# The ten pairs of score maps of a tile in another order in an fp32 transformer trunk kernel

## What is computed

```
def attend(q, k, v):
    s = einsum('bqhgd,bkhd->bhgqk', q, k) * dk ** -0.5
    p = softmax(s, axis=-1)
    return einsum('bhgqk,bkhe->bqhge', p, v)

o_a = attend(q_a, k_a, v_a)                  # 6 heads, 64 wide
o_g = attend(q_g, k_g, v_g)                  # 6 heads, 64 wide
o1 = attend(q_d[..., 0, :], k_d[..., 0, :], v_d)   # 4 differential heads,
o2 = attend(q_d[..., 1, :], k_d[..., 1, :], v_d)   # two maps of 32 each
o_d = rms_norm(o1 - lam * o2, diff_g) * (1.0 - lam_init)
x = x + gate1 * (concat(o_a, o_g, o_d) @ w_out)
```

## Time and profile before

| | |
|---|---|
| median of 3 executions | 1749.79 us (1747.08 to 1751.12) |
| profiled execution: its own time | 1749.15 us |
| its span in the profile | 1747.3 us |
| TensorE matmul busy | 1529.3 us, 88% of the span |
| VectorE busy | 728.0 us, 42% |
| ScalarE busy | 422.4 us, 24% |
| mean granted clock of TensorE | 0.93 |

### The profile page before, as it was taken

One profiled execution on the slowest core, in us unless ns is written; L12 is line 12 of the kernel. 1 busy time (PEld: TensorE's weight loads), 2 busy tenths in 40 slices (PEclk: granted clock), 3 DMA queues, 4 the chain that ended last, 5 costly groups with the idle time before them and its releaser, 6 DMA issues.

```text
span 1747.3 us, 20005 instructions
## 1 busy us (share of the span) xinstructions
PE 1529.3 (88%) x7010; PEld 836.2 (48%) x7010; DVE 728.0 (42%) x1671; ACT 422.4 (24%) x919; POOL 235.2 (13%) x368
## 2 busy tenths in 40 slices
PE   5999988999979899999988998889998975999970
PEld 0134444577756524445523444457776653444430
DVE  0004433567743323344432443356774433433335
ACT  0110111666620001111122111166662000111112
POOL 5111100000020012311031110000002000111114
PEclk8999988799999899999998999879999986999995
DMA  9950008000040478999998000300003006999954
GB/s 313 343 210 11 1 0 277 1 1 2 1 157 29 176 266 262 373 383 382 323 348 315 11 0 1 97 1 2 2 1 109 35 27 219 341 367 368 366 178 183
DMA packets 151834, 283.07 MB, mean 162 GB/s; under 512 B 7104, under 2 KB 95392, under 8 KB 146736
## 3 DMA queue, kind: packets, MB, share of 16 engines
q1 hardware_dynamic: 126832, 197.41, 33.5%
q0 software_dynamic: 24896, 84.28, 12.8%
HBM read 244.45 MB, written 37.32 MB: 161 GB/s over the span
## 4 chain that ended last, share of the span: by engine, by line
PE 76%; DVE 9%; DMA 6%; issue 4%; ACT 2%; POOL 1%; DVEq 1%; SPq 0%; POOLq 0%; ACTq 0%
PE ps L1556 16%; PE ps L1832 16%; PE ps L1501 9%; PE ps L1517 8%; PE ps L1855 7%; PE ps L1631 6%; PE ps L1684 5%; PE ps L1749 4%; DMA ring<-in_w_mod 3%; DMA arena<-in_norm_g 2%; DVE ring L1172 2%; PE ps L1771 1%; PE ps L1626 1%; ACT hT_region L812 1%; PE ps L1578 1%
## 5 line engine op out<-in xcount | busy, mean ns | idle before, releaser
L1556 PE MATMUL ps<-ring,hT_region 128*128 128x512 f32 (+1 forms) x640 | 283.7, 602 | 27.8 <-ACT hT_region L812 27.8
L1832 PE MATMUL ps<-ring,hT_region 128*128 128x512 f32 x624 | 277.6, 598 | 2.0 <-DVE hT_region L1434 1.7
L1556 PEld LDWEIGHTS ps<-ring,hT_region 128*128 128x128 f32 x640 | 125.9, 200 | 167.4 <-issue 166.4
L1517 PE MATMUL ps<-ring,silu_c 128*2 128x512 f32 x384 | 177.4, 624 | 32.4 <-DMA ring<-in_w_mod 29.1
L1172 DVE TENSOR_SCALAR_CACHE_REDUCE ring<-ps 128x768 f32<-128x768 f32 (+1 forms) x168 | 132.7, 820 | 120.3 <-PE ps L1631 97.5
L1832 PEld LDWEIGHTS ps<-ring,hT_region 128*128 128x128 f32 x624 | 116.8, 192 | 135.4 <-issue 135.4
L1749 PE MATMUL ps<-ring,hT_region 128*128 128x384 f32 (+1 forms) x480 | 146.1, 462 | 0.0
L880 ACT ACTIVATE ring<-ring,negm 128x768 f32<-128x768 f32 (+1 forms) x168 | 137.7, 820 | 33.5 <-DVE ring L1172 33.5
L1855 PE MATMUL ps<-arena,work 128*128 128x512 f32 x312 | 140.5, 593 | 1.4 <-DVE work L1457 1.4
L1631 PE MATMUL ps<-arena,qT 64*128 64x384 f32 (+1 forms) x640 | 128.7, 521 | 10.4 <-DVE ring L1172 5.7
L1441 DVE TENSOR_SCALAR work<-work 128x256 f32<-128x256 f32 x39 | 11.5, 294 | 260.0 <-ACT work L966 260.0
(11 more groups left out here) (260 smaller groups left out, 1595.9 us busy)
## 6 DMA issues: line engine op xcount, KB each, us to landing
ring<-in_w_mod SPq DMA_DIRECT2D x24, 2048.0 KB, 12.4
ring<-in_moe_w_gate SPq DMA_DIRECT2D x39, 1024.0 KB, 11.5
ring<-in_moe_w_up SPq DMA_DIRECT2D x39, 1024.0 KB, 13.5
arena<-in_moe_w_down SPq DMA_DIRECT2D x39, 1024.0 KB, 7.9
y_rows<-arena POOLq DMA_DIRECT2D x39, 512.0 KB, 7.9
ring<-in_w_in SPq DMA_DIRECT2D x6, 2048.0 KB, 9.6
arena<-mod_rows POOLq DMA_DIRECT2D x16, 512.0 KB, 11.0
y_rows<-x POOLq DMA_DIRECT2D x1, 7680.0 KB, 21.9
```

The source lines that it names most:

```text
L1517: last = mm(ps[0:2, 2 + j % 2, :], silu_v[:, :, c], w[:, c, :], start=(c == 0), stop=(c == KC - 1))
L1556: last = mm(ps[:, b, 0:n], hT[:, c, t * P:(t + 1) * P], w[:, c, :], start=(c == 0), stop=(c == KC - 1))
L1832: last = mm(ps[:, 2 + i % 2, :], hgT[i % 2][:, c, :], w[:, c, :], start=(c == 0), stop=(c == KC - 1))
```

## The change

The position in the loop and the number of the pair are no longer the same. A table `ORDER` says which pair stands at which position: 0, 6, 1, 2, 3, 7, 4, 8, 9, 5. Pairs 6 and 8, which form no unit of their own, now stand at positions 1 and 7 (before: 6 and 8). The units follow the positions 0, 2, 3, 4, 5, 6, 8, 9 (before: 0 to 5, 7, 9). `COL_OF` says which columns of the output a unit fills. ScalarE's copy of the first four outputs moves by one turn, since the fourth unit comes one turn later.

```
+ORDER = [0, 6, 1, 2, 3, 7, 4, 8, 9, 5]
-UNIT_OF = {0: 0, 1: 1, 2: 2, 3: 3, 4: 4, 5: 5, 7: 6, 9: 7}
+UNIT_OF = {0: 0, 2: 1, 3: 2, 4: 3, 5: 4, 6: 5, 8: 6, 9: 7}
+COL_OF = [0, 1, 2, 3, 6, 4, 7, 5]
+DIFF_UNITS = [u for u in range(N_U) if COL_OF[u] >= 6]
...
-                    if p == 7:
+                    if p == 8:
                         out_copy(t, 0)
...
-                    if p in (6, 8):
+                    if pair in (6, 8):
                         to = dbuf[:, 0:n]
-                        if p == 8:
-                            dve.wait_ge(pt_done[min(t, 1)], units_before(l, t, 6, min(t, 1)) + 1)
+                        if pair == 8:
+                            dve.wait_ge(pt_done[min(t, 1)], units_before(l, t, DIFF_UNITS[0], min(t, 1)) + 1)
...
-                    if k >= 1 and (k - 1) % N_PR >= 6:
+                    if k >= 1 and ORDER[(k - 1) % N_PR] >= 6:
                         difference(k - 1)
...
-                    if p < 6:
+                    if ORDER[p] < 6:
                         pe.wait_ge(exp_done, l * NS + 2 * k + 2)
                         ab = pr[k % 3]
                     else:
-                        pe.wait_ge(d_ready, l * 4 * NT + 4 * t + p - 5)
+                        pe.wait_ge(d_ready, l * 4 * NT + 4 * t + ORDER[p] - 5)
                         ab = [dbuf, pr[k % 3][0]]
...
-                        if p == 9 and b == 0:
+                        if u == 7 and b == 0:
                             pe.wait_ge(oT_ready, l * NT + t)
```

More of the change, by code:

```diff
@@ L878, in probs @@
                     v = pr[k % 3][m][:, 0:P if t == 0 else 768]
-                    c = MAPS * (t % 2) + 2 * p + m
+                    c = MAPS * (t % 2) + 2 * ORDER[p] + m
                     act.activation(v, v, ACT.Exp, bias=negm[:, 2 * (k % 3) + m:2 * (k % 3) + m + 1], scale=-1.0,
@@ L1171, in row_max @@
                         o_ = pr[k % 3][m].rearrange("p (a n) -> p a n", a=2)
-                    ts(o_, i_, -pair_of(p)[4], None, ALU.mult, ALU.min, accum_out=col).then_inc(m_ready, 1)
+                    ts(o_, i_, -pair_of(ORDER[p])[4], None, ALU.mult, ALU.min, accum_out=col).then_inc(m_ready, 1)
                 def probsT(k):
@@ L1185, in difference @@
                     n = P if t == 0 else 768
-                    c = MAPS * (t % 2) + 2 * p
+                    pair = ORDER[p]
+                    c = MAPS * (t % 2) + 2 * pair
                     dve.wait_ge(exp_done, l * NS + 2 * k + 2)
@@ L1193, in difference @@
                     to = p1
-                    if p in (6, 8):
+                    if pair in (6, 8):
                         to = dbuf[:, 0:n]
-                        if p == 8:
-                            dve.wait_ge(pt_done[min(t, 1)], units_before(l, t, 6, min(t, 1)) + 1)
+                        if pair == 8:
+                            dve.wait_ge(pt_done[min(t, 1)], units_before(l, t, DIFF_UNITS[0], min(t, 1)) + 1)
                         elif t >= 1:
                             b = min(t - 1, 1)
-                            dve.wait_ge(pt_done[b], units_before(l, t - 1, 7, b) + 1)
+                            dve.wait_ge(pt_done[b], units_before(l, t - 1, DIFF_UNITS[1], b) + 1)
                         else:
@@ L1616, in scores @@
                     t, p = divmod(k, N_PR)
-                    block_, plane, rows, n, _ = pair_of(p)
+                    block_, plane, rows, n, _ = pair_of(ORDER[p])
                     if p == 0:
@@ L1647, in probsT @@
                     if t == 0:
-                        if p == 7:
+                        if u == 6:
                             pe.wait_ge(qt_evac_d, l * NT + 2)
@@ L1656, in probsT @@
                             pe.wait_ge(pt_evac[b], units_before(l, t, u, b))
-                        if p == 7 and b < 2 and t + 1 < NT:
+                        if u == 6 and b < 2 and t + 1 < NT:
                             pe.wait_ge((qt_evac_d, qt_evac_a)[b], l * NT + t + 2)
-                        if p == 7 and b == 2:
+                        if u == 6 and b == 2:
                             pe.wait_ge(ms_used, l * NT + t)
-                        if p == 9 and b == 0:
+                        if u == 7 and b == 0:
                             pe.wait_ge(oT_ready, l * NT + t)
@@ L1682, in values @@
                     for c, s_ in enumerate(seen):
-                        for m, vc in enumerate(value_columns(u)):
-                            last = mm(ps[64 * m:64 * (m + 1), 7, (u % 4) * P:(u % 4 + 1) * P],
+                        for m, vc in enumerate(value_columns(COL_OF[u])):
+                            last = mm(ps[64 * m:64 * (m + 1), 7, (COL_OF[u] % 4) * P:(COL_OF[u] % 4 + 1) * P],
                                       V[:, s_, vc:vc + 64], w[:, 768 * m + c * P:768 * m + (c + 1) * P],
```

## The result

| | before | after |
|---|---|---|
| median | 1749.01 us (4 runs, 1747.08 to 1751.12) | 1761.72 us (4 runs, 1760.93 to 1763.25) |
| ratio | | 1.0075, 95% interval [1.0059, 1.0091] |
| span of the profiled execution | 1747.3 us | 1761.4 us |
| TensorE matmul busy | 1529.3 us | 1530.9 us |
| attention loop, layer 0 / layer 1 | 197.7 / 196.2 us | 204.6 / 202.8 us |

The change makes the kernel slower by 12.7 us; 1763.0 was forecast. The loops are measured on TensorE's timeline, from the first scores of turn 0 to the first matmul with `w_out`; they grew by 6.9 and 6.6, together 13.5 us of the 14.1 by which the spans differ.

The account below looks back on a forecast made before the run. TensorE was taken to bound full turns of the attention loop, the wait for row maxima the thinner ones. Tile and tail terms summed to +6.77 us a layer, +13.5 for two, giving 1763.0 us (+0.75%), range 1754 to 1769.

Parts of the forecast that it names:

- the score cycle: Scores wait for both row maxima of the turn before, so at least 3.49 us pass from scores to scores.
- Turns 3 and 4, -0.92 each: Tiles 2 to 4: turn 3 loses transposes, turn 4 values; each falls from 4.41 only to 3.49 us.
- turn 8, +1.46: Tiles 2 to 4: turn 8 gains transposes and grows by their whole 1.46 us, with no new wait.
- turn 9, 0: Tiles 2 to 4: turn 9 holds scores and values instead of scores and transposes, and stays 3.58 us.
- turn 1, +0.85: Tiles 2 to 4: values now stand behind the transposes, so turn 1 grows from 3.56 to a full 4.41 us.
- Turn 0, 6.04 with 1.2 idle ahead of the factors: Tiles 2 to 4: factors wait for VectorE's copy of bank 5, 1.2 us idle; turn 0 grows by 1.34 us.
- Tile 1's turn 3, held by the difference for 0.33: Tile 1: turn 2 is only 3.49 us long, so its VectorE difference delays the next row maxima by 0.33 us.
- Tiles 0 and 1, -0.65: First two tiles of a layer: tile 0 gives -0.6 us and tile 1 -0.05 us.
- The tail, +1.99: End of a layer's loop, from scores of turn 49: grows from 12.39 to 14.38 us through uncovered waits.
- The clock rival: Half-idle TensorE in the new tail lowers the clock, about 2 us a layer, +4 in all: 1767 us; chance 0.20.
- The sum: A layer -0.6-0.05+5.43+1.99 = +6.77 us, two layers +13.5: 1762.7, plus 0.6 for the median, forecast as 1763.0 us.
- Interleaving: Rival: separating the differences lets turns 3, 4 and 9 run at TensorE's 2.95 us: 1738 us; chance 0.08.

Follow-up runs that it names:

- neither half of the interleaving: Against the kernel before, only pair 6 moved to position 1: 1750.61 us, ratio 1.0014; only pair 8 separated from pair 9: 1770.43 us, ratio 1.0118.
- the version that beat both kernels: The changed kernel with the factors one turn earlier, in turn 9, and the scores' wait split in halves: 1739.41 us, ratio 0.9948 to the kernel before.

## Why the prediction was right

- **TensorE bounds the loop, and light turns are bound by the score cycle.** Shown: at full clock, light turns of tiles 2 to 4 are 3.49 to 3.58 in every order (3.72 once, with the copy between the row maxima), and without the differences too. No order with an unsplit wait got under 3.49; with the wait split, turns of 2.95 came. Why turn 9 takes 0.09 more than 3.49 was not tried.
- **Turns 3 and 4, -0.92 each; turn 8, +1.46; turn 9, 0; turn 1, +0.85.** Measured 3.49, 3.49, 5.77, 3.58 and 4.41: all as forecast; in the last tile turn 8 grew from 3.49 to 4.95, by the same 1.46.
- **Turn 0, 6.04 with 1.2 idle ahead of the factors.** Measured 6.01 and 1.09, since the factors start 4.12 after the scores instead of 4.19: the copy ends at 4.02 (4.04 forecast), and 0.10 pass to the factors, not 0.15. The factors take 1.89 instead of 1.85, which makes up for part of it. The cause is shown by moving the copy (5.31) and by moving the factors (the wait goes). A tile: forecast 44.4, measured 44.40.
- **Tile 1's turn 3, held by the difference for 0.33.** In layer 1 it took 3.81 instead of 3.49. In VectorE's and TensorE's timelines the row maxima start at 1175.61, 1.92 after the scores instead of 1.59; TensorE's idle time there, 0.71 ahead of the values, is put down to ScalarE's output copy (L904), a wait that the prediction doesn't have. The values start at 1175.97 and take 1.46, so the turn would have ended at 1177.43 by them and ended at 1177.50 by the row maxima: two delays of nearly the same size, of which one was foreseen. In layer 0 the turn took 3.49, behind a turn 12 of 6.04.

```profile
1173.69 1.56 PE L1635 MATMUL ps<-arena,qT 64*128 64x384 f32 x8
...
1174.68 1.02 DVE L1208 SCALAR_TENSOR_TENSOR modrow<-arena,coef,ring 128x768 f32<-128x768 f32 x1
...
1175.61 0.95 DVE L1175 TENSOR_SCALAR_CACHE_REDUCE ring<-ps 128x768 f32<-128x768 f32 x1
```

- **Tiles 0 and 1, -0.65.** Measured from the first scores to turn 0 of tile 2: -1.25 and -0.44. Tile 0 alone gave -0.67 and -0.53, near the -0.6 forecast. Tile 1 gave -0.58 and +0.09 instead of -0.05; the clock moved inside it (below), so that term can't be checked.
- **The tail, +1.99.** Measured +1.64 in layer 1: the first transposes came at 4.95 instead of 5.12, the factors at 6.87 instead of 7.06, and the steps from the last transposes to the end took 4.20 instead of 4.38 (from the rows of layer 1 above: 1332.38, 1337.33, 1339.25, 1342.21 and 1346.41). In layer 0 +2.83, where the clock fell.
- **The clock rival** came in one of two layers. Granted clock of a stretch of the tail in layer 0, and of the same steps in layer 1 (columns as in the earlier trace rows):

```profile
492.00:496.00 4.00, 3.69 (x23) 3.35 (x25) 0.94 (x2) 1.19 (x2) 0.00 (x0) 0.57 0.00 0
1337.00:1341.00 4.00, 3.28 (x44) 3.04 (x44) 1.58 (x3) 1.20 (x2) 0.00 (x0) 1.00 0.00 0
```

It cost 15.22-14.03 = 1.2 us, not the 2 a layer of the rival. What TensorE did just ahead of the last difference doesn't tell the two layers apart. The 4 us from 0.64 after the scores of turn 49, in layer 0 and in layer 1:

```profile
488.00:492.00 4.00, 2.38 (x30) 1.48 (x26) 3.15 (x10) 1.95 (x4) 1.67 (x4) 1.00 0.02 4
1333.02:1337.02 4.00, 2.38 (x30) 1.48 (x26) 3.14 (x10) 1.95 (x4) 1.67 (x4) 1.00 0.00 0
```

Five of the kernels here have this tail (the changed one, both with pair 8 moved, the one with the copy between the row maxima, and the changed one with the split wait). Of their ten tails five took 14.03 or 14.04 us and five 15.22 or 15.23. So in these tails the clock fell five times out of ten, where the prediction gave it 0.20, and each fall cost 1.2 us. The oscillation that the Trainium skill, TensorE: Matmul & The Clock Gate, § A second HAM failure mode: psum-queue depth-cycling, describes did not reach turn 0 of tiles 2 to 4: 44.40 each time, and a granted clock of 1.00 over tile 3.

- **The sum.** The terms gave 13.5, the loops 13.5, the medians 12.7. That the first two agree to a tenth is in part luck: each tail was put 0.35 too long, and the clock fall in layer 0, which the sum doesn't have, added 1.2. Without it the loops would have grown by some 12.3. Added up as the prediction says, 1762.7 and 0.6 are 1763.3, not 1763.0; it changes nothing.
- **Interleaving.** The rule of the Trainium skill, Perfetto Trace Analysis, § Optimization Strategy, that interleaving regimes may improve performance, did not hold here: neither half of the interleaving made the kernel faster by itself, and the version that beat both kernels needed two other edits.

## What to carry to other kernels

In a pipelined loop ask of each turn which engine bounds it, before moving work between turns: evening out an engine that isn't the bound takes work out of full turns and puts it into others, and a turn that is thinned only falls to the length of its dependency cycle. When steps are reordered, look at every wait that isn't edited: "this bank is free" was true long before, and became a wait for a copy that stands last in another engine's turn. Moving the step that needs the bank by one turn can be worth more than any order.

## What the runs showed of the hardware

In tile 1 the clock changed both ways. In layer 0 of the changed kernel the granted clock was 1.00 in turn 10, which took 3.47 us (in the kernel before 0.50 and 4.83), fell again, and turn 12 took 6.04 instead of 3.49. The granted clock over that turn, and over the 4.5 us with half-busy TensorE before it:

```profile
318.00:322.50 4.50, 2.30 (x14) 1.08 (x14) 2.85 (x7) 3.13 (x7) 0.00 (x0) 0.93 0.00 0
322.50:329.00 6.50, 6.04 (x25) 3.86 (x25) 3.27 (x10) 3.34 (x8) 0.00 (x0) 0.52 0.01 1
```

In layer 1 turn 12 took 4.86. In both layers TensorE was idle for 1.53 us ahead of the scores of turn 11 and 1.19 ahead of those of turn 12. Such idle times don't make the clock fall each time: in layer 1 of the kernel before the two turns of the earlier trace rows had 1.55 and 1.56 idle, and the granted clock was 1.00 in them and in the turn behind, which took 4.42. It had come up just ahead of them (0.50 from 1154.20 to 1156.00). What decides between the two cases was not tried. In turn 0 and the light turns of tiles 2 to 4, with idle times of 1.09 and 0.47, it never fell.
